# Layer 0: the last modulation section's eight products moved from the mix-in into the mix-out

## The chip, the cores and the metric

The kernel runs on one core of one Trainium2 chip. The metric is the device time of one execution in microseconds; a lower one is better. Three runs of the kernel before are shown, with their median.

## The reference: what is computed

Two layers work on a context of 256 tokens and a latent stream of 1024 tokens, all of width 1024 in float32. Only what bears on the change is shown:

```python
for l in range(DEPTH):
    sh1, sc1, g1, sh2, sc2, g2 = adaln(c, w_ada[l], b_ada[l])        # silu(c) @ w_ada + b_ada, cut in 6
    csh1, csc1, cg1, csh2, csc2, cg2 = adaln(c_ctx, w_ada[l], b_ada[l])
    p = modulate(x, sh1, sc1) @ w_in[l]                              # the mix-in
    ...                                                              # retention and convolution
    mix_x = mixer_output(...)                                        # the mix-out: normalise, gate, @ w_out
    x = layer_norm(DEEPNORM_ALPHA * x + g1 * mix_x, ln1_w[l], ln1_b[l])
    x = layer_norm(DEEPNORM_ALPHA * x + g2 * mlp(modulate(x, sh2, sc2)), ln2_w[l], ln2_b[l])
```

Each of the six sections of the modulation is a vector of 1024 numbers for the latent and one for the context: a product of (2 x 1024) with (1024 x 1024). Section 5 is the gate g2 of the MLP and the last to be used: it is read after the mix-out.

## The kernel before, in words

Tokens lie in ten tiles of 128 (two of context, eight latent). Every float32 product is done in three passes over a high and a low part. A layer has three stages: the mix-in (projection with w_in, retention, convolution), the mix-out (projection with w_out, residual, first layer norm) and the MLP. Each engine has its own program in order; semaphores join them. SP issues the loads and stores of rows on its DMA queue; ScalarE issues the weight loads on its own queue and rounds the high parts; GpSimd makes the low parts.

**Modulation in layer 0.** Sections 0 and 1 are computed at the start. Sections 2 to 5 (`ADA_OWN`) are computed within the mix-in, in eight pieces each, a piece being 128 rows of w_ada (512 KB). `ada_piece_load` (L1106 to L1111) has ScalarE issue two loads of 256 KB into `ada_half`, which is part of `plain_words`; there is room for one piece, so ScalarE waits (`ada_used`) until TensorE has used the one before. `ada_products` (L612 to L616) is the visit of TensorE: four small products into bank 7, in the trace eight matmuls of L615. After the eighth, VectorE adds the bias in four additions (`ada_bias`, L1478 to L1484) and SP stores the section in DRAM with four stores (`ada_store`, L659 to L663); `ada_stored` waits until they have landed.

**The mix-in's order** comes from `mix_in_plan`, which runs through 64 projection steps and puts the other work between them: a visit every second step, retention's scores and values, evacuations, taps of the convolution. When the steps are over, retention's last quarter is done ("late" scores and values), after a scan on VectorE.

**The mix-out's order.** TensorE goes through steps st = 0 to 12. In a step it transposes the convolution columns of tile st (L987, from `cv_in`), transposes the mixed rows of tile st - 2 (L996), and projects tile st - 3 onto the first 512 columns. The second 512 columns follow in a loop of their own, `beside_ln1`, with the first layer norm beside it. What a tile passes through is:

- SP loads retention rows and columns (`rows_of`, L724 and L725) for tile j once the columns' transposes of tile j - 2 are done, gate rows (L729) after the mix of tile j - 2, and the residual rows of tile j - 2 (`residual`, L787) once its mixed transposes are done; these stand in one queue in that order.
- VectorE centres and scales the heads (L1655 to L1685), GpSimd applies weight, bias and gate (L1399 to L1404), and then TensorE may do the mixed transposes. ScalarE applies silu to the gates, to the turned columns (L1242) and makes the high part (L1247); VectorE makes the low part (L1668), and TensorE projects.
- VectorE adds the projection to the residual (`combine`, L1647 and L1648; in the second half L1708 and L1709), which frees the bank: the second half's tile j waits for the sum of tile j - 2 (`z_read`).

Between the halves VectorE waits for `gate_in`, which counts four loads of SP: the gate for the second half (L804) and the first layer norm's weight and bias (L806):

```python
                for cd in range(2):
                    sp.dma_start(g_in[:, cd, :], ada_d[l, cd, 2 * D + 512:3 * D].partition_broadcast(P)).then_inc(S["gate_in"], 16)
                for i, r in enumerate((ln1_w, ln1_b)):
                    sp.dma_start(ln1_rows[:, i, :], r[l].partition_broadcast(P)).then_inc(S["gate_in"], 16)
...
                dve.wait_ge(S["gate_in"], s0["gate_in"] + 64)
                dve.wait_ge(S["mod2_in"], s0["mod2_in"] + 64)
                nc.vector.tensor_scalar(modc[:, 3, :, :], modc[:, 3, :, :], 1.0, None, ALU.add).then_inc(S["one_added"], 1)
```

Of the kernel before, what the change touches and what calls it, by code (L numbers as in the profile page):

```python
# [28 lines left out]
P = 128  # L29
D = 1024  # L30
KT = D // P
# [38 lines left out]
ADA_FIRST = 2  # L70
ADA_OWN = list(range(ADA_FIRST, 6))
# [10 lines left out]
def mix_in_plan(layer):  # L82
# [36 lines left out]
    plan, evacs, posts, ready = [], list(range(len(steps))), [i for i, st in enumerate(steps) if st[0] == "Q"], []  # L119
    scored, valued, scanned, evac_at, taps = set(), set(), set(), {}, []  # L120
    n = 0
    pieces = [(s, k) for s in (() if layer else ADA_OWN) for k in range(KT)]
    finished, stored, pause, consumed = [], [], 2, False
    while n < len(steps) or posts or len(valued) < PAIRS * len(tiles) or pieces or finished or stored:
        if n < len(steps):
# [38 lines left out]
        k = 0  # L164
# [23 lines left out]
        elif pieces:  # L188
            s, k = pieces.pop(0)
# [69 lines left out]
def build(nc, x, c, ctx, c_ctx, w_ada, b_ada, w_in, rate_f, rate_b, gn_w, gn_b, conv_w, conv_b,  # L259
          cln_w, cln_b, w_out, ln1_w, ln1_b, w_ff1, w_ff2, ln2_w, ln2_b, const_cols, const_rope, out):  # L260
    es = ExitStack()
    with es:
# [112 lines left out]
        ada_half = [plain[:, at + SLOTS:at + H_WORDS] for at in (H_AT, H_AT + H_WORDS)]  # L375
# [277 lines left out]
        def _(sp):  # L653
# [11 lines left out]
            def ada_stored(sections):  # L665
                sp.wait_ge(ada_st, 64 * (sections - ADA_FIRST))
# [34 lines left out]
            for l in range(DEPTH):  # L701
# [65 lines left out]
                        ada_bias_load(a[1])  # L767

                if l == 0:
                    ada_stored(ADA_OWN[-1] + 1)  # L770
                for par in range(2):
                    sp.wait_ge(S["g_st"][par], s0["g_st"] + 16 * (n * PAIRS // 2))
                    sp.wait_ge(S["o_st"][par], s0["o_st"] + 16 * (n * PAIRS // 2))
# [28 lines left out]

                for cd in range(2):
                    sp.dma_start(g_in[:, cd, :], ada_d[l, cd, 2 * D + 512:3 * D].partition_broadcast(P)).then_inc(S["gate_in"], 16)  # L804
                for i, r in enumerate((ln1_w, ln1_b)):
                    sp.dma_start(ln1_rows[:, i, :], r[l].partition_broadcast(P)).then_inc(S["gate_in"], 16)  # L806

# [39 lines left out]
        def _(pe):  # L847
# [25 lines left out]
            for l in range(DEPTH):  # L873
                s0, T = BEFORE[l], tiles_of(l)
                n = len(T)
                steps, plan = PLANS[l]
                qn, bs, as_ = ([sum(st[0] == kind for st in steps[:i]) for i in range(len(steps) + 1)] for kind in "QBA")

                def project_step(i):
                    kind, p, t = steps[i]  # L880
# [32 lines left out]
                for a in plan:  # L913
                    if a[0] == "proj":
                        i = a[1]
                        if i < PROJ_BANKS:
                            continue

                        j = i - PROJ_BANKS
                        if steps[j][0] == "Q" and has_query(l, steps[j][2]):  # L920
                            pe.wait_ge(S["evac_q"], s0["evac_q"] + queries_before(l, qn[j + 1]))
                        elif steps[j][0] == "Q":
                            pe.wait_ge(S["v_ready"], s0["v_ready"] + qn[j + 1])
                        elif steps[j][0] == "B":
                            pe.wait_ge(S["sig_done"], s0["sig_done"] + bs[j + 1])
                        else:
                            pe.wait_ge(S["glu_done"], s0["glu_done"] + as_[j + 1])
                        project_step(i)
                    elif a[0] == "post":
                        q = qn[a[1]]  # L930
                        pe.wait_ge(S["rot_done"], s0["rot_done"] + 2 * (q + 1))
                        pe.wait_ge(S["vdec_done"], s0["vdec_done"] + q + 1)
                        if q:
                            pe.wait_ge(S["u_evac"], s0["u_evac"] + q)
                        src = qk_rot[:, q % 2, :]
                        if has_query(l, steps[a[1]][2]):
                            for h in range(2):
                                nc.tensor.transpose(ps_tr[:, h * P:(h + 1) * P], src[:, h * P:(h + 1) * P], ident)
                        nc.tensor.matmul(ps_u[:, 0:2 * P], src[:, P:2 * P], v_dec, start=True, stop=True).then_inc(S["u_done"], 1)  # L939
                    elif a[0] == "scores":  # L940
                        _, p, t, late = a
                        r = row_of(l, p, t)
                        pe.wait_ge(S["qd_done"], s0["qd_done"] + r + 1)
                        if late:
                            pe.wait_ge(S["evac_q"], s0["evac_q"] + n * PAIRS)
                            pe.wait_ge(S["prob_done"], s0["prob_done"] + r - 1)
                        elif r:
                            pe.wait_ge(S["prob_done"], s0["prob_done"] + r)
                        nc.tensor.matmul(ps_scores(r, late), qk_t[:, t, 1, :], q_diag[:, r % 2, :], start=True, stop=True).then_inc(S["score_done"], 1)
                    elif a[0] == "values":  # L950
                        _, p, t, late = a
                        r = row_of(l, p, t)
                        pe.wait_ge(S["prob_done"], s0["prob_done"] + r + 1)
                        pe.wait_ge(S["sd_done"], s0["sd_done"] + r + 1)
                        ps_o = ps_values(r, late)
                        if late:
                            pe.wait_ge(S["evac_q"], s0["evac_q"] + n * PAIRS)
                            pe.wait_ge(S["conv_op"], s0["conv_op"] + 4 * TAPS * len(chunks_of(l)))
                            pe.wait_ge(S["comb_b"], s0["comb_b"] + r - 1)
                        elif r:  # L960
                            pe.wait_ge(S["comb_b"], s0["comb_b"] + r)
                        for h in range(2):
                            nc.tensor.matmul(ps_o[:, h * DK:(h + 1) * DK], probs[:, r % 2, h * P:(h + 1) * P], v_sb[:, t, h * DK:(h + 1) * DK], start=True, stop=True)  # L963
                        nc.tensor.matmul(ps_o[:, P:3 * P], qk_t[:, t, 0, :], s_diag[:, r % 2, :], start=True, stop=True).then_inc(S["val_done"], 1)  # L964
                    elif a[0] == "ada":
                        _, s, k = a
                        pe.wait_ge(piece_in, 32 * (KT * (s - ADA_FIRST) + k + 1))
                        if k == 0:
                            pe.wait_ge(ada_row, s)
                        ada_products(pe, s, k, lambda q: ada_half[q // 2][:, (q % 2) * 2 * P:(q % 2 + 1) * 2 * P])  # L970

                chunks = chunks_of(l)
                ps_c, ps_z, ps_m = banks[4:6], banks[2:4], banks[0:2]
                for st in range(n + 3):
                    if st < n:
                        pe.wait_ge(S["cv_in"][st % 2], s0["cv_in"] + 16 * (st // 2 + 1))
                        if st >= 2:
                            pe.wait_ge(S["cnorm"], s0["cnorm"] + st - 1)
                        elif st == 0:
                            pe.wait_ge(S["evac_q"], s0["evac_q"] + n * PAIRS)  # L980
                            pe.wait_ge(S["post_evac"], s0["post_evac"] + n * PAIRS)
                            pe.wait_ge(S["u_evac"], s0["u_evac"] + NT * PAIRS)
                            pe.wait_ge(S["prob_done"], s0["prob_done"] + n * PAIRS)
                            pe.wait_ge(S["comb_b"], s0["comb_b"] + n * PAIRS)
                            pe.wait_ge(S["conv_op"], s0["conv_op"] + 4 * TAPS * len(chunks))
                        for ct in range(4):
                            mm = nc.tensor.transpose(ps_c[st % 2][:, ct * P:(ct + 1) * P], cv_in[:, st % 2, ct, :], ident)  # L987
                        mm.then_inc(S["cvt_done"], 1)
                    j = st - 2
                    if 0 <= j < n:  # L990
                        pe.wait_ge(S["mix_a"], s0["mix_a"] + j + 1)
                        pe.wait_ge(S["cnorm"], s0["cnorm"] + j + 1)
                        if j:
                            pe.wait_ge(S["mix_lo"], s0["mix_lo"] + j)
                        for k in range(KT):
                            mm = nc.tensor.transpose(ps_m[k // 4][:, (k % 4) * P:(k % 4 + 1) * P], X[:, T[j], k * P:(k + 1) * P], ident)  # L996
                        mm.then_inc(S["mixtr_done"], 1)
                    j = st - 3
                    if j >= 0:
                        pe.wait_ge(S["mix_lo"], s0["mix_lo"] + j + 1)  # L1000
                        if j >= 2:
                            pe.wait_ge(S["z_read"], s0["z_read"] + j - 1)
                        project(pe, l, IN_UNITS, T[j], ps_z[j % 2][:, :], j == 0, j == n - 1, S["z_done"])
# [88 lines left out]
        def _(act):  # L1092
# [29 lines left out]
            for l in range(DEPTH):  # L1122
# [22 lines left out]
                for a in plan:  # L1145
# [73 lines left out]
                    elif a[0] == "values":  # L1219
# [7 lines left out]
                            last = nc.scalar.activation(s_diag[r64, r % 2, h * P:(h + 1) * P].rearrange("p (a b) -> p a b", b=DK), state[r64, t, :, :], ACT.Copy)  # L1227
                        last.then_inc(S["sd_done"], 1)

                for st in range(n + 2):  # L1230
                    j = st - 1
                    if 0 <= j < n:
                        act.wait_ge(S["g_in"][j % 2], s0["g_in"] + 16 * (j // 2 + 1))
# [235 lines left out]
        def _(dve):  # L1469
# [50 lines left out]
            for l in range(DEPTH):  # L1520
# [169 lines left out]
                for st in range(1, n + 4):  # L1690
# [7 lines left out]
                        low_part(st - 2)  # L1698
                    if st < n:
                        variance(st)  # L1700
                dve.wait_ge(S["gate_in"], s0["gate_in"] + 64)
                dve.wait_ge(S["mod2_in"], s0["mod2_in"] + 64)
                nc.vector.tensor_scalar(modc[:, 3, :, :], modc[:, 3, :, :], 1.0, None, ALU.add).then_inc(S["one_added"], 1)
# [112 lines left out]
```

## Time and profile before

| | |
|---|---|
| median of 3 runs | 2971.93 us (2970.01 to 2973.99) |
| profiled execution | 2972.73 us, its span 2970.7 us |
| TensorE busy | 2729.2 us (92%) |
| VectorE busy | 1937.0 us (65%) |
| ScalarE busy | 714.6 us (24%) |
| GpSimd busy | 1067.2 us (36%) |
| chain that ended last | TensorE 81%, VectorE 7%, GpSimd 4%, DMA 3%, issue 2% |

The profile is of one execution. Times are microseconds from the span's start. PE is TensorE's matmuls and PEld its weight loads, DVE is VectorE, ACT ScalarE, POOL GpSimd; SPq and ACTq are DMA issues on SP's and ScalarE's queues. A line number is that of the kernel. The granted clock is given in parts of the full one (2.4 GHz), so 0.50 is 1.2 GHz.

### The profile page before, as it was taken

Reading aid. Unit: us, or ns where it says so; the run is one execution under the profiler, and the core shown is the slowest. Engines: PE = TensorE matmul, PEld = TensorE weight load, DVE = VectorE, ACT = ScalarE, POOL = GpSimd, SP = SyncE. Lnnn points to the kernel's source line nnn. Section 1 sums busy time; section 2 is a strip of 40 time slices with the busy share of each in tenths; the row PEclk is TensorE's granted clock in tenths of the full one; section 3 lists DMA queues with packets and bytes.
Section 4 is the critical chain, followed back from the end, with each engine's and each line's share of the span. In section 5 each row is a group of like instructions: output and inputs, shape, how many; then the busy total and the mean of one; then the engine's idle time right before and its main releaser. Section 6 shows DMA issues by size and latency. Waiting matters only on the chain.

```text
span 2970.7 us, 36867 instructions
## 1 busy us (share of the span) xinstructions
PE 2729.2 (92%) x13212; PEld 2224.5 (75%) x13212; DVE 1937.0 (65%) x3223; ACT 714.6 (24%) x1454; POOL 1067.2 (36%) x973
## 2 busy tenths in 40 slices
PE   5999898697999999999999599998688999999996
PEld 3777676576888888888887487787567888888885
DVE  4778785667677677667768788772655544454556
ACT  3222234434211111110111323334423111111111
POOL 1244354455111111111112644553663233332325
PEclk9999999799999999999999799999898999999998
DMA  8222222531122222222220211111512111111111
GB/s 242 88 75 73 86 86 77 140 125 36 53 82 71 71 71 77 68 82 71 71 41 25 92 48 59 60 48 41 154 61 71 43 56 42 49 49 42 56 42 64
DMA packets 246650, 214.59 MB, mean 72 GB/s; under 512 B 60384, under 2 KB 203280, under 8 KB 246544
## 3 DMA queue, kind: packets, MB, share of 16 engines
q10 hardware_dynamic: 139776, 117.46, 13.2%
q1 hardware_dynamic: 106768, 95.77, 10.8%
q8 instruction: 60, 0.98, 0.1%
q14 instruction: 46, 0.38, 0.0%
HBM read 190.56 MB, written 22.63 MB: 72 GB/s over the span
## 4 chain that ended last, share of the span: by engine, by line
PE 81%; DVE 7%; POOL 4%; DMA 3%; issue 2%; SPq 1%; ACT 1%; ACTq 0%; POOLq 0%; DVEq 0%
PE bank L535 14%; PE bank L537 14%; PE bank L536 14%; PE bank L1030 9%; PE bank L1031 9%; PE bank L1032 9%; PE bank L896 2%; PE bank L897 2%; PE bank L898 2%; PE bank L615 1%; PE bank L964 1%; PE bank L939 1%; PE bank L963 1%; DMA work<-conv_columns 1%; DMA plain_words<-in_w_ada 1%
## 5 line engine op out<-in xcount | busy, mean ns | idle before, releaser
L1460 POOL TENSOR_TENSOR w_lo<-raw,w_hi 128x1024 fp32r<-128x1024 f32 x120 | 288.1, 2402 | 1115.0 <-ACT w_hi L1294 1115.0
L1030 PE MATMUL bank<-x_hl,w_hi 128*128 128x512 f32 (+1 forms) x1280 | 474.8, 371 | 0.0
L1031 PE MATMUL bank<-x_hl,w_hi 128*128 128x512 f32 (+1 forms) x1280 | 472.7, 369 | 0.0
L1032 PE MATMUL bank<-x_hl,w_lo 128*128 128x512 f32 (+1 forms) x1280 | 472.1, 369 | 0.0
L1753 DVE TENSOR_TENSOR work<-work,bank 128x512 f32<-128x512 f32 x576 | 389.9, 685 | 122.4 <-PE bank L537 111.5
L1729 DVE TENSOR_TENSOR work<-work 128x512 f32<-128x512 f32 (+1 forms) x160 | 158.0, 988 | 471.2 <-ACT work L1282 471.1
L535 PE MATMUL bank<-w_hi,h_hi 128*128 128x512 f32 x1152 | 450.6, 391 | 7.4 <-DVE work L1753 5.5
L537 PE MATMUL bank<-w_hi,h_lo 128*128 128x512 f32 x1152 | 448.8, 390 | 0.0
L536 PE MATMUL bank<-w_lo,h_hi 128*128 128x512 f32 x1152 | 448.8, 390 | 0.0
L1634 DVE SCALAR_TENSOR_TENSOR bank<-work,bank 128x512 f32<-128x512 f32 (+1 forms) x580 | 407.0, 702 | 18.9
L1294 ACT ACTIVATE w_hi<-raw 128x1024 fp32r<-128x1024 f32 x120 | 126.8, 1059 | 783.1 <-PE bank L537 584.7
L1030 PEld LDWEIGHTS bank<-x_hl,w_hi 128*128 128x128 f32 x1280 | 242.7, 190 | 45.2 <-ACT work L1282 5.2
L1032 PEld LDWEIGHTS bank<-x_hl,w_lo 128*128 128x128 f32 x1280 | 242.5, 189 | 40.5
L1031 PEld LDWEIGHTS bank<-x_hl,w_hi 128*128 128x128 f32 x1280 | 242.7, 190 | 39.7
L535 PEld LDWEIGHTS bank<-w_hi,h_hi 128*128 128x128 f32 x1152 | 216.6, 188 | 59.1 <-DVE work L1753 9.2
L537 PEld LDWEIGHTS bank<-w_hi,h_lo 128*128 128x128 f32 x1152 | 216.6, 188 | 45.0
L536 PEld LDWEIGHTS bank<-w_lo,h_hi 128*128 128x128 f32 x1152 | 216.7, 188 | 44.5
L531 POOL TENSOR_TENSOR w_lo<-raw,w_hi 128x1024 fp32r<-128x1024 f32 x52 | 125.3, 2409 | 281.8 <-ACT w_hi L515 281.8
L1751 DVE TENSOR_TENSOR bank<-bank,work 128x512 f32<-128x512 f32 x320 | 221.5, 692 | 0.2
L535 PE MATMUL bank<-w_hi,x_hl 128*128 128x512 f32 (+1 forms) x536 | 211.9, 395 | 1.8 <-POOL w_lo L531 1.7
L1282 ACT ACTIVATE work<-bank 128x512 f32<-128x512 f32 (+1 forms) x160 | 88.6, 554 | 519.0 <-PE bank L1032 517.6
L536 PE MATMUL bank<-w_lo,x_hl 128*128 128x512 f32 (+1 forms) x536 | 206.3, 385 | 0.0
(141 smaller groups left out, 4397.2 us busy)
## 6 DMA issues: line engine op xcount, KB each, us to landing
raw<-in_w_ff ACTq DMA_DIRECT2D x128, 512.0 KB
work<-in_w_ada SPq DMA_DIRECT2D x48, 512.0 KB
raw<-in_w_in ACTq DMA_DIRECT2D x64, 256.0 KB
plain_words<-in_w_ada ACTq DMA_DIRECT2D x64, 256.0 KB
raw<-in_w_in ACTq DMA_DIRECT2D x16, 512.0 KB
plain_words<-in_w_ada SPq DMA_DIRECT2D x16, 512.0 KB, 12.4
raw<-in_w_out ACTq DMA_DIRECT2D x16, 512.0 KB
gate_rows<-work SPq DMA_DIRECT2D x72, 64.0 KB, 1.6
```

Source lines behind the costliest of these rows:

```text
L535: nc.tensor.matmul(out_ps, hi, whi, start=first, stop=False)
L536: nc.tensor.matmul(out_ps, hi, wlo, start=False, stop=False)
L537: return nc.tensor.matmul(out_ps, lo, whi, start=False, stop=last)
L1030: nc.tensor.matmul(o, slot(mlp_slot(l, f), 0)[:, wc], x_hi[:, k, cols], start=k == 0, stop=False)
L1031: nc.tensor.matmul(o, slot(mlp_slot(l, f), 0)[:, wc], x_lo[:, k, cols], start=False, stop=False)
L1032: mm = nc.tensor.matmul(o, slot(mlp_slot(l, f), 1)[:, wc], x_hi[:, k, cols], start=False, stop=k == KT - 1)
L1294: nc.scalar.activation(slot(mlp_slot(l, sl), 0), raw[:, un % 2, :], ACT.Copy).then_inc(w_high, 1)
L1460: nc.gpsimd.tensor_tensor(slot(mlp_slot(l, sl), 1), raw[:, un % 2, :], slot(mlp_slot(l, sl), 0).bitcast(F32), ALU.subtract).then_inc(w_rea ...
L1634: nc.vector.scalar_tensor_tensor(into, taps_in, wcol, acc_ps, ALU.mult, ALU.add).then_inc(S["conv_op"], 1)
L1729: nc.vector.tensor_tensor(a32, a32, a32, ALU.mult).then_inc(S["h_sq"], 1)
L1751: nc.vector.tensor_tensor(gated, gated, gate2[:, cond_of(t), hc], ALU.mult).then_inc(S["y_gated"], 1)
L1753: nc.vector.tensor_tensor(X[:, t, hc], X[:, t, hc], gated, ALU.add).then_inc(S["y_read"], 1)
```

## The change

Section 5 leaves the plan of the mix-in. In the mix-out of layer 0 TensorE visits one piece in each of the steps 1 to 8, behind the mixed transposes of that step and ahead of its projection. ScalarE loads piece 0 before its first step and piece st - 1 at the head of steps 2 to 8, each after a wait for the visit before. VectorE adds the bias after the last low part and sum of the first half, ahead of its wait for `gate_in`. SP stores the section and waits for the stores to land between the gate's two loads and the two loads of the first layer norm's rows.

```diff
@@ -119,7 +119,7 @@
     plan, evacs, posts, ready = [], list(range(len(steps))), [i for i, st in enumerate(steps) if st[0] == "Q"], []
     scored, valued, scanned, evac_at, taps = set(), set(), set(), {}, []
     n = 0
-    pieces = [(s, k) for s in (() if layer else ADA_OWN) for k in range(KT)]
+    pieces = [(s, k) for s in (() if layer else ADA_OWN[:-1]) for k in range(KT)]
     finished, stored, pause, consumed = [], [], 2, False
     while n < len(steps) or posts or len(valued) < PAIRS * len(tiles) or pieces or finished or stored:
         if n < len(steps):
@@ -767,7 +767,7 @@
                         ada_bias_load(a[1])
 
                 if l == 0:
-                    ada_stored(ADA_OWN[-1] + 1)
+                    ada_stored(ADA_OWN[-1])
                 for par in range(2):
                     sp.wait_ge(S["g_st"][par], s0["g_st"] + 16 * (n * PAIRS // 2))
                     sp.wait_ge(S["o_st"][par], s0["o_st"] + 16 * (n * PAIRS // 2))
@@ -802,6 +802,9 @@
 
                 for cd in range(2):
                     sp.dma_start(g_in[:, cd, :], ada_d[l, cd, 2 * D + 512:3 * D].partition_broadcast(P)).then_inc(S["gate_in"], 16)
+                if l == 0:
+                    ada_store(ADA_OWN[-1])
+                    ada_stored(ADA_OWN[-1] + 1)
                 for i, r in enumerate((ln1_w, ln1_b)):
                     sp.dma_start(ln1_rows[:, i, :], r[l].partition_broadcast(P)).then_inc(S["gate_in"], 16)
 
@@ -875,6 +878,9 @@
                 n = len(T)
                 steps, plan = PLANS[l]
                 qn, bs, as_ = ([sum(st[0] == kind for st in steps[:i]) for i in range(len(steps) + 1)] for kind in "QBA")
+
+                def half_columns(q):
+                    return ada_half[q // 2][:, (q % 2) * 2 * P:(q % 2 + 1) * 2 * P]
 
                 def project_step(i):
                     kind, p, t = steps[i]
@@ -967,7 +973,7 @@
                         pe.wait_ge(piece_in, 32 * (KT * (s - ADA_FIRST) + k + 1))
                         if k == 0:
                             pe.wait_ge(ada_row, s)
-                        ada_products(pe, s, k, lambda q: ada_half[q // 2][:, (q % 2) * 2 * P:(q % 2 + 1) * 2 * P])
+                        ada_products(pe, s, k, half_columns)
 
                 chunks = chunks_of(l)
                 ps_c, ps_z, ps_m = banks[4:6], banks[2:4], banks[0:2]
@@ -995,6 +1001,12 @@
                         for k in range(KT):
                             mm = nc.tensor.transpose(ps_m[k // 4][:, (k % 4) * P:(k % 4 + 1) * P], X[:, T[j], k * P:(k + 1) * P], ident)
                         mm.then_inc(S["mixtr_done"], 1)
+                    if l == 0 and 1 <= st <= KT:
+                        s, k = ADA_OWN[-1], st - 1
+                        pe.wait_ge(piece_in, 32 * (KT * (s - ADA_FIRST) + k + 1))
+                        if k == 0:
+                            pe.wait_ge(ada_row, s)
+                        ada_products(pe, s, k, half_columns)
                     j = st - 3
                     if j >= 0:
                         pe.wait_ge(S["mix_lo"], s0["mix_lo"] + j + 1)
@@ -1227,7 +1239,13 @@
                             last = nc.scalar.activation(s_diag[r64, r % 2, h * P:(h + 1) * P].rearrange("p (a b) -> p a b", b=DK), state[r64, t, :, :], ACT.Copy)
                         last.then_inc(S["sd_done"], 1)
 
+                if l == 0:
+                    act.wait_ge(ada_used, KT * ADA_OWN[-1])
+                    ada_piece_load(ADA_OWN[-1], 0)
                 for st in range(n + 2):
+                    if l == 0 and 2 <= st <= KT:
+                        act.wait_ge(ada_used, KT * ADA_OWN[-1] + st - 1)
+                        ada_piece_load(ADA_OWN[-1], st - 1)
                     j = st - 1
                     if 0 <= j < n:
                         act.wait_ge(S["g_in"][j % 2], s0["g_in"] + 16 * (j // 2 + 1))
@@ -1698,6 +1716,8 @@
                         low_part(st - 2)
                     if st < n:
                         variance(st)
+                if l == 0:
+                    ada_bias(ADA_OWN[-1])
                 dve.wait_ge(S["gate_in"], s0["gate_in"] + 64)
                 dve.wait_ge(S["mod2_in"], s0["mod2_in"] + 64)
                 nc.vector.tensor_scalar(modc[:, 3, :, :], modc[:, 3, :, :], 1.0, None, ALU.add).then_inc(S["one_added"], 1)
```

## Rows read from the trace of the kernel before

**Rows 1.** The page: the span.

```profile
span 2970.7 us, 36867 instructions
```

**Rows 2.** Windows: each engine's busy time and instructions, granted clock, DMA share, GB/s.

```profile
400.00:440.00 40.00, 40.00 (x200) 31.24 (x199) 30.74 (x56) 12.87 (x39) 26.12 (x39) 1.00 0.29 89
...
540.00:560.00 20.00, 6.49 (x27) 5.00 (x25) 13.25 (x28) 5.72 (x8) 10.44 (x8) 0.50 0.56 125
...
660.00:680.00 20.00, 20.00 (x94) 16.67 (x93) 13.98 (x30) 4.47 (x4) 15.27 (x9) 1.00 0.00 1
```

**Rows 3.** The chain that ended last, mix-in: start, us, what.

```profile
426.66 0.54 PE bank L615 x8
...
486.18 0.55 PE bank L615 x8
...
504.61 0.45 ACTq L1111
```

**Rows 4.** The timeline, end of the mix-in: start, us, engine, line, out<-in, [idle before <- releaser].

```profile
504.21 0.84 ACTq L1111 DMA_DIRECT2D plain_words<-in_w_ada  x2
...
505.16 0.63 ACT L1217 ACTIVATE work<-work 64x128 f32<-64x128 f32 x2 [0.69 <-issue]
...
516.84 1.03 PE L615 MATMUL bank<-plain_words,work 128*2 128x256 f32 x8
...
519.20 0.42 DVE L1593 TENSOR_TENSOR work<-bank,work 128x256 f32<-128x256 f32 x1
...
519.54 1.71 DVE L1483 TENSOR_TENSOR work<-bank,work 2x256 f32<-2x256 f32 x4
...
520.93 1.17 PE L964 MATMUL bank<-work 128*128 128x256 f32 x2
...
521.28 1.16 SPq L663 DMA_DIRECT2D ada_rows<-work  x4
```

**Rows 5.** The timeline, TensorE's transposes in the mix-out.

```profile
556.83 1.11 PE L987 MATMUL bank<-work 128*128 128x128 f32 x4 [12.13 <-DMA work<-conv_columns]
...
567.03 1.12 PE L987 MATMUL bank<-work 128*128 128x128 f32 x4 [7.38 <-DMA work<-conv_columns]
...
584.89 1.09 PE L996 MATMUL bank<-work 128*128 128x128 f32 x8 [1.43 <-POOL work L1404]
...
592.78 0.66 PE L987 MATMUL bank<-work 128*128 128x128 f32 x4 [1.33 <-DMA work<-conv_columns]
...
608.58 1.09 PE L996 MATMUL bank<-work 128*128 128x128 f32 x8 [0.86 <-POOL work L1404]
...
615.72 0.66 PE L987 MATMUL bank<-work 128*128 128x128 f32 x4 [0.56 <-DMA work<-conv_columns]
```

**Rows 6.** The chain that ended last, mix-out: a load of columns.

```profile
560.55 6.44 DMA work<-conv_columns
```

**Rows 7.** The timeline, ScalarE's queue beside it.

```profile
561.41 0.41 ACTq L459 DMA_DIRECT2D raw<-in_w_out  x1
```

**Rows 8.** DMA issues: line's tiles, count, KB each, median us from issue to landing.

```profile
retention_rows<-work SPq DMA_DIRECT2D x72, 64.0 KB, 1.5
...
work<-conv_columns SPq DMA_DIRECT2D x18, 256.0 KB, 4.5
...
work<-in_x SPq DMA_DIRECT2D x8, 512.0 KB, 3.6
```

**Rows 9.** The timeline, between the mix-out's halves.

```profile
633.91 0.43 SPq L806 DMA_DIRECT2D work<-in_ln_b  x1
...
643.73 0.69 DVE L1648 SCALAR_TENSOR_TENSOR work<-work,bank 128x512 f32<-128x512 f32 x1
...
648.77 0.70 DVE L1708 TENSOR_TENSOR bank<-bank,work 128x512 f32<-128x512 f32 x1 [4.28 <-PE bank L537]
...
654.04 0.39 PE L535 MATMUL bank<-h_hi,x_hl 128*128 128x512 f32 x1
```

**Rows 10.** DMA of L806, the first layer norm's rows: issue to landing.

```profile
DMA to landing us min/median/max: 6.4/7.2/8.5
```

## The prediction

> **What bounds the kernel now.** I read the page first: a span of 2970.7 us [rows 1]; the profiled execution took 2972.73, 0.8 above the median of the runs shown (2971.93). Then the windows around the two stages that the change touches [rows 2]. In the mix-in TensorE is busy for every microsecond of 400 to 440, at the full clock. Early in the mix-out it is busy 6.5 of 20 us, at a granted clock of 0.50, and the DMA engines' share has doubled to 0.56. From 660 to 680, in the mix-out's second half, TensorE is full again and VectorE busy 14 of 20. So the products leave a stage in which TensorE sets the pace and enter one in which it waits. The question is what they bring along: eight loads of 512 KB on ScalarE's queue, four additions on VectorE, four stores on SP's queue.
>
> **What the mix-in gives back.** Section 5 has eight visits of TensorE. In the chain that ended last the first five stand as pieces of 0.54 or 0.55 us, the first at 426.66, the fifth at 486.18 [rows 3]; TensorE has no gap there, so all five come off the end: 5 x 0.546 = 2.7 us. The sixth visit is not in that chain, but the load behind it is: ScalarE issues it at 504.21 (0.84 us), its next copy (L1217) comes 0.69 us late for "issue", and a matmul waits for that copy [rows 3, 4]: 0.7 us. The seventh visit and its load lie in waits of both engines for others, and the eighth visit (1.03 us, from 516.84) runs while VectorE still computes the scan; the first product with the mask comes at 519.20. VectorE's four additions (1.71 us at 519.54) hold back its second mask product, but TensorE is then on the first tile's values until 522.1, at half clock. The four stores (1.16 us) go ahead of a store whose data come later [rows 4]. I cost all that at nothing; the cover is the scan and TensorE's own row of products, and without it the gain would be up to 1.7 us more. Mix-in: 2.7 + 0.7 = 3.4 us gained, bounds 2.7 and 5.1.
>
> **What the mix-out pays: the loads.** Its steps form a ring. The mixed transposes of tile j (L996) end; SP then loads residual rows, retention rows and convolution columns, 1 MB, for later tiles; TensorE projects a tile (from 585.98, the end of the transposes at 584.89, to 591.45, where its wait begins: 5.5 us) and wants the columns of tile j+3 for L987. It waits for them 12.13 us before 556.83, 7.38 before 567.03, 1.33 before 592.78 and 0.56 before 615.72 [rows 5]. A load of columns takes 4.5 us in the middle [rows 8]. One took 6.44 [rows 6]: issued at 560.55, while a w_out unit, also 512 KB, was asked for on ScalarE's queue at 561.41 [rows 7]. So 1.9 us is the price of 512 KB at that phase, 0.9 us behind the columns' own issue, and ScalarE reaches the head of a step, where it will issue a piece, at about that point.
>
> Piece 0 is visited in front of the wait of 12.13 us: nothing, even if it is late. Piece 1 follows a unit on its queue right before SP's rows for tile 2, the ones of that wait: +1.9, bounds 0 and 1.9. Piece 2 comes behind the unit of 561.41, whose traffic has stretched that load already: +0.5, bounds 0 and 1.9. Pieces 3 and 4 come while TensorE projects, and a wait of 1.43 us for GpSimd follows: nothing, bound 1.9. Piece 5 falls on the columns for which TensorE waits at 592.78: +1.9, bounds 0 and 1.9. Pieces 6 and 7 meet the end of a load that is wanted just when the projection ends: +0.4 together, bounds 0 and 2.8.
>
> A rule bears on this and speaks against the change. By the Trainium skill (DMA: Bandwidth & Descriptors, Queues, rings and completion order) SP's and ScalarE's queues own one ring each on the same 16 engines, and an engine takes turns between the rings packet by packet. By that rule every piece would stretch the columns of its step, which as an estimate puts the sum at rival D's; the row of 6.44 us agrees, and the other columns, alone in their time, can't show it.
>
> **The visits.** That of step 3, behind the transposes that follow 567.03, runs at half clock, as the one at 516.84 did (1.03 us); it moves the first projection, and with it VectorE, GpSimd and the transposes at 584.89 that wait for GpSimd: +1.0, bounds 0.5 and 1.0. Those of steps 1 and 2 are under the waits for columns. Of the other five, at 0.55 each, four have a wait behind them (1.43, 1.33, 0.86, 0.56) and one has none [rows 5]: +0.6, bounds 0 and 2.8. Mix-out: 1.9 + 0.5 + 1.9 + 0.4 + 1.0 + 0.6 = 6.3 us lost.
>
> **The end of the first half.** Here a wait is added. Before, SP issued the last of ln1's rows at 633.91, to land 6.4 to 8.5 us later, so by 642.4; VectorE asks for them (gate_in) after its last first-half sum, ended at 644.42, and starts the second half's first at 648.77, when TensorE is done with it: 6 us of slack [rows 9, 10]. After, the section's stores stand before those loads in SP's queue: they wait for VectorE's additions, and the loads wait until the stores have landed. In before's times: 644.42 + 1.71 additions = 646.1; + 1.16 for four issues = 647.3; + 1.5 to land (the 64 KB stores' median, an estimate for 2 KB) = 648.8; the second ln1 load goes out 0.45 later, 649.25; + 6.4 = 655.65 [rows 4, 8, 10]. VectorE stands in that wait, and behind it are the one-add (0.2) and the sum of tile 0 (1.4), which gives TensorE its bank back: 657.25. TensorE wants it for the third tile at 654.04 [rows 9]. Stall: 3.2 us. Bounds: with the 3.6 us of a 512 KB load of x [rows 8], 0.4; with 8.5, 5.3. Behind TensorE wait the layer's remaining eight projections, without a gap in before; VectorE has room there [rows 2] and catches up, TensorE does not.
>
> **Sum.** -3.4 + 6.3 + 3.2 = +6.1 us: 2972.73 becomes 2978.8 for a profiled execution, 2978.0 as a median.
>
> **Rivals.** (A) The pieces fit between SP's bursts, as the engines' share leaves over 40% free [rows 2]: only the visits (1.6) and the end are paid, -3.4 + 1.6 + 3.2 = +1.4, 2973.3. For it: pieces 3 to 7 are asked for late in a burst; against it: the 6.44. (B) Not slower: ln1's rows, with no gate rows ahead of them in the queue, land as fast as an x load. The end then costs 0.4, and with A's loads -3.4 + 1.6 + 0.4 = -1.4, 2970.5. It decides from a landing below 4 us on. Against it: no such load took less than 6.4. (C) The piece itself is late. It is asked for one step before its visit, and the next only after that visit: the ring is 1.8 us from the transposes to its issue, 0.4 for the second half, 8.0 to land behind 1 MB (what ln1's rows take behind theirs, within their 6.4 to 8.5), 0.55 for the visit, 10.75 in all against (608.58 - 584.89) / 3 = 7.9 now [rows 5]. Six steps x 2.85 = 17.1, in place of the 2.9 of the later visits and pieces 5 to 7: +20.3, and with 6.4 to land +10.7; I take the middle, 15, 2986.9. Against it: 512 KB alone take 3.6. (D) Every piece stretches the columns of its step. Piece 2 pays 1.4 more, pieces 3 and 4 together 3.8 - 1.43, pieces 6 and 7 together 3.8 - 0.86 - 0.4; less the 0.65 by which each of the four loads ends before a projection and a visit do: 1.4 + 2.4 + 2.5 - 2.6 = 3.7 more, +9.8, 2981.7. For it: the one row that shows two queues at once; against it: two thirds of a load of columns may be through when the piece's data start.
>
> **Chances.** Forecast 0.53, A 0.14, B 0.10, C 0.08, D 0.15. The forecast's own range is 2974.5 to 2981.5 (piece 5 and the landing of the rows at their bounds). The range for 8 in 10 reaches to B below and to most of C above: 2970 to 2986. A measurement of this kernel tells about 0.2% (5.9 us) from no change, so slower begins at 2977.9, at the forecast: half of its cases, nearly all of C and D and little of A, 0.50. Faster would need -5.9, which only B with the full gain of the tail and every visit covered comes near: 0.05. Within: 0.45.
>
> **What would show it.** After the change: no L615 between 426 and 517; the chain about 3.4 us earlier when the mix-out starts; columns that land in 6 us and more where pieces are issued, with longer waits of L987 at the third and the seventh tile; VectorE idle before its first second-half sum for a DMA of ln1's rows, and a hole of about 3 us in TensorE behind the second half's second tile. If the mix-in gives less than 2.5, or the hole is missing, or TensorE waits at L615 for pieces, the step of that name is wrong.

## The result and the profile after

The changed kernel takes 2978.74 us in the median of 13 runs (2976.62 to 2980.67), the one before 2972.96 in 13 of its own; the ratio is 1.002, with an interval of 1.0012 to 1.0028. That is 5.8 us more, where +6.1 was forecast. A second comparison, on another chip, gave 1.0028 (1.0015 to 1.004), +8.3 us (7.9 by the medians). The profiled execution took 2978.58 us, its span is 2976.6.

The chain that ended last, in the changed kernel, where the mix-out starts (start, us, what); it answers to [rows 3 and 6]:

```profile
547.92 0.61 SPq L724
548.57 7.23 DMA work<-conv_columns
...
555.84 1.12 PE bank L993 x4
556.96 1.72 PE bank L1002 x8
...
559.56 6.51 DMA work<-conv_columns
...
566.11 1.11 PE bank L993 x4
567.23 1.71 PE bank L1002 x8
568.93 0.96 PE bank L615 x8
569.90 0.73 PE bank L535
```

The columns of the third tile now take 7.23 us. In the chain of before the same load is:

```profile
552.03 4.76 DMA work<-conv_columns
```

The load of the fourth, 6.44 before, takes 6.51. Then a visit is itself in the chain (L615, at half clock), between the mixed transposes and the projection. The timeline of ScalarE's queue shows what stands beside the first of these loads:

```profile
547.33 0.46 ACTq L459 DMA_DIRECT2D raw<-in_w_out  x1
547.83 0.46 ACTq L1123 DMA_DIRECT2D plain_words<-in_w_ada  x1
548.32 0.45 ACTq L1123 DMA_DIRECT2D plain_words<-in_w_ada  x1
```

Piece 1 goes out as SP asks for the rows. The timeline of TensorE's transposes (L993 is L987 of before, L1002 is L996), which answers to [rows 5]:

```profile
539.80 1.94 PE L993 MATMUL bank<-work 128*128 128x128 f32 x8 [1.04 <-DVE work L1623]
...
555.84 1.12 PE L993 MATMUL bank<-work 128*128 128x128 f32 x4 [13.14 <-DMA work<-conv_columns]
...
566.11 1.11 PE L993 MATMUL bank<-work 128*128 128x128 f32 x4 [6.49 <-DMA work<-conv_columns]
...
585.12 1.09 PE L1002 MATMUL bank<-work 128*128 128x128 f32 x8 [0.92 <-POOL work L1422]
...
592.29 0.66 PE L993 MATMUL bank<-work 128*128 128x128 f32 x4
```

At the seventh tile, where before waited 1.33 us for columns, there is no wait at all (592.29), although a piece is loaded beside it. The wait for GpSimd at 585.12 is 0.92 in place of 1.43.

Between the halves the chain is this (answers to [rows 9 and 10]; pieces of one line stand one below the other):

```profile
644.41 0.71 DVE bank L1665
...
645.75 0.40 DVE work L1501
...
647.04 0.44 DVE work L1501
...
647.49 0.27 SPq L663
...
648.41 2.54 DMA ada_rows<-work
...
650.97 0.36 SPq L809
...
651.37 5.55 DMA work<-in_ln_b
...
656.94 0.17 DVE work L1723
...
657.15 0.71 DVE bank L1728
...
657.88 0.70 DVE work L1729
...
658.62 0.50 PE bank L535
```

It is the queue as forecast: the last sum of the first half, four additions, four stores, their landing, the rows, their landing, the one-add, the sum, and only then TensorE's third tile. TensorE's own row shows the hole, and the windows what comes behind it (each engine's busy time, with the number of its instructions, in the order PE, PEld, DVE, ACT, POOL; then granted clock, DMA share, GB/s):

```profile
658.62 0.50 PE L535 MATMUL bank<-h_hi,x_hl 128*128 128x512 f32 x1 [3.37 <-DVE work L1729]
```

```profile
655.00:660.00 5.00, 1.63 (x8) 1.16 (x7) 2.92 (x6) 0.00 (x0) 0.72 (x1) 1.00 0.46 147
660.00:665.00 5.00, 5.00 (x17) 3.94 (x16) 3.30 (x9) 1.24 (x1) 1.10 (x2) 0.66 0.00 0
665.00:670.00 5.00, 5.00 (x24) 4.14 (x23) 3.10 (x7) 0.71 (x1) 0.73 (x2) 1.00 0.01 3
...
658.60:660.10 1.50, 1.48 (x6) 1.24 (x7) 1.46 (x3) 0.00 (x0) 0.00 (x0) 1.00 0.00 0
660.10:663.50 3.40, 3.40 (x9) 2.64 (x8) 3.20 (x9) 0.00 (x0) 0.56 (x2) 0.50 0.00 0
```

In the five microseconds from 660 on, TensorE is busy all the time but runs 17 products in place of the 24 of the next window, at a mean granted clock of 0.66. The last two rows divide it: for 1.5 us after the hole TensorE still has the full clock, then 3.4 us of work are granted 0.50, then it is full again. That was not in the forecast. From 660 to 680 the kernel before had 94 matmuls at 1.00 [rows 2]; the changed one has 83 at 0.91.

**Stages.** One execution is a coarse measure: what comes before the change varies by some 5 us from profile to profile (the last visit of section 4 starts at 407.47, 412.81 and 408.48 us in three profiles of the kernel before). So the stages are compared by their lengths, between marks that every kernel has: the last visit of section 4 (m), the first transposes of columns (a), those of the third tile (c), the last mixed transposes (x), VectorE's last sum of the second half (z: the last L1709 of before). The kernel before was profiled two more times (below), the changed one once more.

| | m to a | a to c | c to x | x to z | m to z |
|---|---|---|---|---|---|
| before, three profiles | 135.3, 136.1, 134.6 | 14.1, 14.2, 14.6 | 74.1, 72.2, 72.9 | 70.9, 70.9, 71.4 | 294.4, 293.3, 293.5 |
| changed, two profiles | 132.0, 132.0 | 16.0, 15.9 | 76.5, 76.6 | 75.8, 76.1 | 300.3, 300.5 |
| rows first, three | 131.4, 131.6, 131.8 | 16.1, 15.9, 16.1 | 74.7, 76.1, 77.8 | 70.7, 70.6, 70.6 | 292.9, 294.2, 296.4 |
| + small loads | 131.5 | 14.7 | 75.6 | 71.4 | 293.2 |
| + small visits | 131.2 | 16.0 | 78.6 | 70.5 | 296.4 |
| + both | 131.8 | 14.6 | 74.5 | 70.6 | 291.5 |
| changed, hole filled | 131.8 | 16.2 | 77.6 | 74.3 | 299.9 |
| rows first, three stay | 134.6 | 13.9 | 75.8 | 70.5 | 294.8 |
| rows first, piece 1 late | 131.6 | 14.0 | 79.9 | 71.1 | 296.5 |

By the means, the changed kernel gains 3.4 us to a (before's mean 135.3, its own 132.0), loses 1.7 to c, 3.5 to x and 4.9 to z: 6.7 us in all by the column m to z, against 5.8 and 8.3 timed.

Where the 3.5 us from c to x go can be read from TensorE's busy time. These are the windows of that stage in before and in the changed kernel, and the same stretch of the changed kernel for the visits' line alone (L615: PE, PEld):

```profile
556.83:630.94 74.11, 60.71 (x296) 49.38 (x296) 58.26 (x114) 38.32 (x80) 56.58 (x46) 0.90 0.48 148
555.84:632.37 76.53, 65.87 (x352) 50.35 (x352) 56.01 (x114) 38.51 (x80) 54.07 (x45) 0.90 0.56 183
555.84:632.37 76.53, 5.13 (x56) 0.74 (x56) 0.90 0.56 183
```

TensorE is busy for 60.7, 61.3 and 61.7 us in the three profiles of before and for 65.9 and 66.6 in the two of the changed kernel: 5.0 us more, about what its seven visits there take. It stands idle for the rest, 11.8 us in the mean before and 10.3 after: 1.5 us less, although seven pieces are loaded beside it. In these profiles the stage is longer by the visits' own work, of which shorter waits cover less than a third, and not by longer waits for columns.

### The profile page after: what moved, and what is told of

It reads as the page before. It is cut to its first block, busy times and chain, and to the rows that moved or that the text cites. A ratio compares the mean times of both kernels' runs of the same rounds, so it can differ in the third digit from the quotient of the medians.

```text
span 2976.6 us, 36867 instructions
## 1 busy us (share of the span) xinstructions
PE 2737.2 (92%) x13212; PEld 2233.4 (75%) x13212; DVE 1940.0 (65%) x3223; ACT 715.4 (24%) x1454; POOL 1066.4 (36%) x973
## 4 chain that ended last, share of the span: by engine, by line
PE 80%; DVE 7%; POOL 5%; DMA 3%; issue 2%; SPq 1%; ACT 1%; ACTq 0%; POOLq 0%; DVEq 0%
PE bank L535 14%; PE bank L537 14%; PE bank L536 14%; PE bank L1042 9%; PE bank L1043 9%; PE bank L1044 9%; PE bank L902 2%; PE bank L903 2%; PE bank L904 2%; PE bank L615 1%; PE bank L970 1%; DMA work<-conv_columns 1%; PE bank L945 1%; DMA plain_words<-in_w_ada 1%; PE bank L969 1%
## 5 line engine op out<-in xcount | busy, mean ns | idle before, releaser
L535 PE MATMUL bank<-w_hi,x_hl 128*128 128x512 f32 (+1 forms) x536 | 212.3, 396 | 1.4 <-POOL w_lo L531 1.2
L537 PE MATMUL bank<-w_hi,x_hl 128*128 128x512 f32 (+1 forms) x536 | 206.6, 385 | 0.0
```

The lines of the kernel that those rows point to most:

```text
L535: nc.tensor.matmul(out_ps, hi, whi, start=first, stop=False)
L537: return nc.tensor.matmul(out_ps, lo, whi, start=False, stop=last)
```

## Experiments

The theory after the result: the end of the first half costs a hole and, behind it, half clock; the rest of the mix-out's loss is the traffic of the pieces and the visits. The rival: the hole belongs to VectorE's additions or to the traffic, and the traffic is hidden.

**Rows first.** The two loads of ln1's rows go ahead of the section's stores on SP.

```diff
-                if l == 0:
-                    ada_store(ADA_OWN[-1])
-                    ada_stored(ADA_OWN[-1] + 1)
                 for i, r in enumerate((ln1_w, ln1_b)):
                     sp.dma_start(ln1_rows[:, i, :], ...).then_inc(S["gate_in"], 16)
+                if l == 0:
+                    ada_store(ADA_OWN[-1])
+                    ada_stored(ADA_OWN[-1] + 1)
```

> The changed kernel with SP's two loads of ln1's rows issued ahead of the section's stores. Theory (the rows behind the stores make a stall of 3.4 us, and the half clock that follows it costs 1.7 more): about 5 us come back, so +0.9 us against the kernel before, no wait for a DMA in front of VectorE's first sum of the second half, no hole in TensorE, granted clock 1.00 from 650 to 680. Rival (VectorE's four additions or the pieces' traffic make that hole): it stays, +4 to +6 us against before.

Measured: 1.0011 of the kernel before (1.0002 to 1.002), +3.3 us (2.4 by the medians). The stage tells more than the time. Its windows:

```profile
655.00:660.00 5.00, 5.00 (x24) 4.14 (x23) 3.10 (x7) 0.57 (x1) 3.12 (x3) 1.00 0.21 84
660.00:665.00 5.00, 5.00 (x24) 4.14 (x23) 3.10 (x7) 0.86 (x2) 0.21 (x1) 1.00 0.01 3
```

24 matmuls in each, at full clock. From x to z it takes 70.7 us where the changed kernel takes 75.8: the hole and the half clock behind it, 5.1 us, are gone, while VectorE's additions stayed where they were. The rival on the additions and the traffic falls. The time did not come down to +0.9 but to +3.3 us, with an interval of +0.6 to +6.

**The loads and the visits, each made small on top of that.** These three kernels leave out part of section 5, so that they tell of the time alone.

```diff
+                    few = P if s < ADA_OWN[-1] else 16
-                    act.dma_start(ada_half[half], w_ada[l, k * P:(k + 1) * P, at:at + 512]).then_inc(piece_in, 16)
+                    act.dma_start(ada_half[half][0:few, :], w_ada[l, k * P:k * P + few, at:at + 512]).then_inc(piece_in, 16)
```

```diff
             for q in range(4):
+                w = 8 if s == ADA_OWN[-1] else 2 * P
-                mm = nc.tensor.matmul(ada_bank(s)[32 * q:32 * q + 2, 0:2 * P], cond_s[:, k, :], columns(q), ...)
+                mm = nc.tensor.matmul(ada_bank(s)[32 * q:32 * q + 2, 0:w], cond_s[:, k, :], columns(q)[:, 0:w], ...)
```

> As e1_rows_first, but each of section 5's loads fetches 16 of 128 partitions, an eighth of the bytes; the products run over old data in the rest. Theory (the pieces stretch the loads of columns that TensorE waits for, above all that of the third tile, 7.23 us against 4.76): 2 to 3 us less than e1_rows_first, about -1.5 us against before, and the third tile's columns land in 4.8 us again. Rival (the traffic is hidden and the mix-out's loss is that of the visits): within 0.7 us of e1_rows_first.

> As e1_rows_first, but the products of section 5 have 8 columns in place of 256 (the section is not computed); loads, waits and counts stay. Theory (the visit at half clock moves the first projection by 1 us, of the others about half is under waits): 1.5 to 2.5 us less than e1_rows_first. Rival (all visits lie under waits for columns or GpSimd): within 0.7 us of it; rival (visits cost their full 0.55 each): 4 us less.

> As e1_rows_first, with both the small loads and the small products. What is left is what the mix-in gives back: theory -3 us against the kernel before (chain at the mix-out's start 3.0 us earlier in the changed kernel), and the gains of e2 and e3 add up to that of this one. Rival (loads and visits cover each other: a visit costs nothing where the columns are late anyway): this one gains clearly less than the sum of the two.

Measured: 1.0003 (0.9994 to 1.0012) with small loads, 1.0005 (0.9996 to 1.0014) with small visits, 0.9998 (0.9989 to 1.0007) with both; the intervals overlap. Against the rows first that is 2.4, 1.8 and 3.9 us less; the first two add up to about the third, as the theory has it, but each is uncertain by some 3 us. The stages are clear in one place: a to c is 14.7 and 14.6 us where the loads are small and 15.9 to 16.2 in the seven profiles with whole loads at their place. So the traffic of piece 1 costs the third tile's columns 1.4 us or a little more; as the chain of the small loads has it:

```profile
549.68 5.38 DMA work<-conv_columns
...
558.83 5.65 DMA work<-conv_columns
```

5.38 us in place of 7.23, not the 4.8 expected. For c to x the grain of a single profile (74.7 to 77.8 in three of one kernel) is larger than what was sought: 75.6 and 74.5 with small loads against a mean of 76.2 (rows first) is in the expected direction, 78.6 with small visits against it: TensorE was busy for 63.5 us there, 2.4 less than in the changed kernel's first profile, but idle for 15.0, of which 13.0 in waits for columns. So what the small visits gave back was lost again in waits, in this one profile. The visits' work is in the changed kernel's stage, as its rows show; what the stage would be without them is not shown. With both small, the mix-in's gain is the only large thing left and the kernel should have been 3 us faster than before; the ratio allows -3.3 to +2.1 us, the stages give 2.2 us less than before's mean (291.5 against 293.7).

**The kernel before, profiled again, and the rows first a second time.**

> The kernel before once more, for a second profile of it. Every theory: from the last visit of section 4 to the first transposes of columns 135.2 us as in the first profile, within 0.5; to the third tile's columns 14.1; to the last mixed transposes 74.1; to the last first-product of the second half 70.9. How far these differ is the grain with which stages can be compared.

Its stages are in the table, 0.9 and 1.9 us off the first profile's in two of the four where 0.5 was expected. The three profiles of before differ by 1.5, 0.5, 1.9 and 0.5 us in the four stages. That is the grain.

> e1_rows_first once more, since its interval was 2 per mille wide. Theory: 0 to +2 us against the kernel before by its stages (mix-in 3.3 to 3.9 less, third tile's columns 2.0 more, rest of the first half 0.5 to 2.4 more, second half as before). Rival (something outside these stages costs 2 us more): +3 us again.

Measured: 1.0017 (1.0008 to 1.0026), +5.1 us of 2972 (4.1 by the medians), where its stages give +0.5 against before's mean. That is on the rival's side, and more than its +3. In this profile TensorE also waits 0.87 us for piece 2 itself, at 569.31.

**The hole filled.** In the changed kernel TensorE runs 13 products that nobody reads before it waits for the third tile's bank.

```diff
+                    if l == 0 and j == 2:
+                        for i in range(13):
+                            nc.tensor.matmul(banks[5][:, :], x_hi[:, 0, T[0] * P:(T[0] + 1) * P], slot(slot_of(l, IN_UNITS + 4), 0)[:, 0:512], start=True, stop=True)
                     if j < n:
                         pe.wait_ge(S["z_read"], s0["z_read"] + n + j - 1)
```

> The changed kernel, the hole kept, but TensorE runs 13 products of 128x512 into a bank that nobody reads, some 3 us, before it waits for the third tile's bank. Theory (the hole of 3.4 us is followed by 3.4 us at half clock, which costs 1.7): the third tile starts when it did (4.6 us later than in before), the granted clock stays 1.00 from 658 on, and 1.7 us come back: +4 us against before. Rival (TensorE's later steps are late for VectorE's or GpSimd's sake, not the clock's): no gain, or a loss.

TensorE's timeline and the windows, of this kernel:

```profile
659.43 3.11 PE L1019 MATMUL bank<-h_hi,x_hl 128*128 128x512 f32 x13
663.04 0.50 PE L535 MATMUL bank<-h_hi,x_hl 128*128 128x512 f32 x1 [0.51 <-DVE work L1732]
```

```profile
660.00:665.00 5.00, 4.49 (x21) 3.37 (x20) 3.47 (x8) 0.00 (x0) 0.26 (x2) 1.00 0.28 105
665.00:670.00 5.00, 5.00 (x24) 4.14 (x23) 3.89 (x9) 1.24 (x1) 0.99 (x2) 1.00 0.01 3
```

The wait is as long (the third tile starts at 663.04, 0.74 after VectorE's L1732 begins, as 658.62 was after 657.88), but the clock stays at 1.00, and x to z is 74.3 us, 1.5 to 1.8 less than in the changed kernel. So of the 4.9 us of that stage some 1.6 are the clock and the rest is the wait. The rival on VectorE and GpSimd falls. As a time it can't be told: 1.0033 (1.0017 to 1.005) beside 1.0028 for the changed kernel elsewhere.

**Three pieces stay in the mix-in's tail, five move, to steps 3 to 7.**

```diff
+KEPT = 3
...
-    pieces = [(s, k) for s in (() if layer else ADA_OWN[:-1]) for k in range(KT)]
+    pieces = [(s, k) for s in (() if layer else ADA_OWN) for k in range(KT if s < ADA_OWN[-1] else KEPT)]
...
-        elif pieces:
+        elif pieces and (pieces[0][0] < ADA_OWN[-1] or n >= 62):
...
-                    if l == 0 and 1 <= st <= KT:
-                        s, k = ADA_OWN[-1], st - 1
+                    if l == 0 and KEPT <= st < KT:
+                        s, k = ADA_OWN[-1], st
...
```

ScalarE's loads are moved in the same way.

> As e1_rows_first, but three of the eight pieces stay at the end of the mix-in, where the visits lie in waits, and five are moved, to steps 3 to 7. No piece then stands before SP's rows of the third tile. Theory: that load of columns takes 4.8 us again (2.0 saved), the mix-in gives back 2.2 to 2.7 in place of 3.4, and the kernel is the fastest of all, -1 us against before. Rival (any piece costs the columns 2 us somewhere): no better than e1_rows_first.

Half of it held. With no piece before the third tile's rows, a to c is 13.9 us, the 2.0 saved. But the mix-in gives back only 0.7 (134.6), not 2.2 to 2.7. Its chain shows why in part: the first of the three visits stands in it again, and so does an issue of a piece ahead of the scan.

```profile
493.78 0.54 PE bank L616 x8
...
509.24 0.45 ACTq L1124
```

These are 1.1 of the 2.7 us by which it falls short of the changed kernel; the rest is not explained. Timed it was 1.002 (1.0011 to 1.003): no better than the rows first, and not the fastest of all.

**Both kernels timed beside each other, the rows first a third time, and piece 1 later.**

> The kernel before as a kernel of its own, timed against itself beside the three below. Every theory: ratio 1.000 within its interval; what it deviates is what the others' differences are worth.

0.9999 (0.999 to 1.0008): a kernel timed against itself shows an uncertainty of a tenth of a per cent, 3 us.

> The changed kernel once more, on the same chip as the next. Theory: +5 to +6.5 us against before; mix-out's second half 75.8 us long again, with the hole behind its second tile and half clock after it. Rival (the hole was that one execution's): second half 71 us.

> The rows first, on the same chip as the changed kernel. Theory from the stages of the profiles: 5 us less than after_again, between 0 and +1.5 against before. Rival (two timed comparisons gave +2.4 and +4.1 in place of it): only 2 to 3 us less than after_again, with no stage of the profile to show the rest.

1.0028 (1.0015 to 1.004) and 1.0017 (1.0008 to 1.0026). The first is above the +5 to +6.5 expected, which lie in its interval; the second is above the +1.5. The second half is 76.1 and 70.6 us long, so the hole is no accident and its removal is shown. The difference of the times is 3.3 us (3.7 by the medians), between what the stages say (mean 294.5 against 300.4, 5.9) and the rival's 2 to 3, and nearer to the rival's.

```diff
-                    if l == 0 and 2 <= st <= KT:
+                    if l == 0 and 3 <= st <= KT:
...
                         last.then_inc(S["mix_hi"], 1)
+                    if l == 0 and st == 2:
+                        act.wait_ge(ada_used, KT * ADA_OWN[-1] + 1)
+                        ada_piece_load(ADA_OWN[-1], 1)
```

> As e1_rows_first, but piece 1 is asked for after ScalarE has made the first tile's high part, some 9 us later, so that it stands behind SP's rows of the third tile. Theory (its traffic stretches those columns by 2.0 us): first to third columns' transposes take 14.1 us again in place of 16.0; the fourth's columns are a little later; 1 to 2 us less than e1_rows_first. Rival (the stretch only moves to the fourth tile's columns, for which TensorE waits as well): no gain.

No gain, as the rival has it, but by another wait: a to c is 14.0 us, as expected, and c to x 79.9, three more than any mean. The timeline of this kernel:

```profile
560.32 0.82 ACTq L1123 DMA_DIRECT2D plain_words<-in_w_ada  x2
561.38 0.41 ACTq L459 DMA_DIRECT2D raw<-in_w_out  x1
...
566.59 1.03 PE L615 MATMUL bank<-plain_words,work 128*2 128x256 f32 x8 [7.83 <-DMA plain_words<-in_w_ada]
567.55 1.11 PE L993 MATMUL bank<-work 128*128 128x128 f32 x4
```

Now TensorE waits 7.83 us for the piece itself, in front of the columns' transposes. A piece asked for 6 us before its visit is waited for, as in rival C. The time is 1.0017 (1.0008 to 1.0026).

## Why the prediction was right, and which steps were off

The forecast of +6.1 against +5.8 measured rests on three terms. The first is exact; the second is 1.1 us too large and the third 1.7 too small, and these two errors nearly cancel. That the total came out so close is in part luck, all the more as the second comparison gave +8.3.

**The mix-in, 3.4 forecast:** 3.4 (135.3 to 132.0), and 3.5 to 4.1 in the eight other profiles with the same mix-in. Right in its size, within the grain. Its place is right too: in both chains of the changed kernel no visit and no issue of a piece is left between m and a, where the first chain of before has five visits and an issue [rows 3].

**The first half, 6.3 forecast:** 5.2 (1.7 + 3.5). Piece 1, +1.9 forecast, is right: 1.7 by the stage; the load itself took 7.23 us in place of 4.76. The Trainium skill (DMA: Bandwidth & Descriptors, Queues, rings and completion order) has the engines take turns between the two queues; the trace agrees in that the columns slow down beside the other queue's load, with 7.23 us beside a whole piece and 5.38 beside a small one. It does not show the turns themselves. Piece 2, +0.5, cost nothing in that profile (6.51 against 6.44). The step-3 visit at half clock is in the chain with 0.96 us, as forecast. Mis-sized are the two sums behind it. Pieces 2 to 7 were put at 2.8 us of longer waits; TensorE's waits from c to x became 1.5 us shorter, and at the seventh tile, where piece 5 was put at 1.9, no wait for columns is left in the first profile (592.29) and 0.2 us in the second. The visits were put at 1.6 us, most of them under waits; they are 5.0 us of more work, of which the shorter waits cover 1.5. So 4.4 forecast and 3.5 measured agree more by their sum than by their terms. That the pieces are free there can't be said either. In one profile of the rows first the fifth tile's columns took 7.31 us and TensorE waited 1.65 for them; with small visits the waits grew, and with small loads and small visits the stage was 74.5 us long against 73.1 before, within the grain. So rival A fell at piece 1 and is undecided for the others. C and D each ask for more than the stages show.

**The end, 3.2 forecast:** a hole of 3.37 us, and 4.9 for the stage. The chain of causes was right, and so was its length, 12.8 us from the last sum's end to TensorE's third tile; but that is luck in part, as its two landings were off in opposite directions: the stores took 2.54 where 1.5 was estimated, the rows 5.55 after their issue where 6.4 was taken from [rows 10]. What failed is the step "Behind TensorE wait the layer's remaining eight projections, without a gap in before", which leaves the stall at its own length: they do run without a gap, but from 1.5 us on for 3.4 us at half clock. The missing term is 1.6 us, shown by the filled hole. The Trainium skill (TensorE: Matmul & The Clock Gate, Part 1: The HAM clock gate) says that an idle engine's clock falls to 1.2 GHz; the trace agrees, with 17 matmuls at a mean of 0.66 from 660 to 665 behind the hole, 24 at 1.00 where there was none, and 1.00 throughout where it was filled. Rival B needed a landing below 4 us; the rows took 5.55.

**The range.** The forecast's own range was given as 2974.5 to 2981.5, "piece 5 and the landing of the rows at their bounds". With these two terms at their bounds it would be 2973.3 to 2980.1. The measured 2978.7 lies in both.

**What stays open.** With the rows first, three timed comparisons say 3.3, 5.1 and 5.1 us more than before (2.4, 4.1 and 4.2 by the medians), each interval clear of zero; the stages of the same kernel's three profiles average 0.8 more (294.5 against 293.7), with 3.5 us between the highest and the lowest, and the spans 1.5 more (2973.6 against 2972.1). Three executions can't settle a difference of 3 us, and outside m to z the three profiles are in the mean 0.7 us longer than before's. Where the rest is spent is not known. That version is no slower than the changed one and probably faster, but none of the versions beats the kernel before.

## What to carry to other kernels

Work that is moved off a full engine takes its loads, additions and stores along, and each joins a queue that others wait in. Here 3.4 us of products were given back and 10 us paid, half of it by two small loads that had been free as long as they stood ahead of the stores: before a dependent store is put into a queue, look at what is behind it. Price a hole of this length in TensorE as its length and what the clock costs behind it. And read a stage's loss as busy time and idle time apart: here the one had grown by the visits while the other had shrunk.

## What had not been expected of the hardware

A wait of 3.4 us in TensorE was followed by seven fewer matmuls in the next 5 us (17 against 24), so nearly half as much again was lost as the wait itself. The clock did not fall in the wait but 1.5 us after TensorE had started again, in both profiles of the changed kernel. Four stores of 2 KB landed 2.54 us after the last was issued, longer than the median of the 64 KB stores (1.5). And a load of 512 KB on ScalarE's queue, asked for 0.7 us ahead of SP's 256 KB of columns, made those land in 7.23 us in place of 4.76.
